# Page registers held longer, index scores packed on the array, and a reordered beginning in a two-layer decoder step

## The chip, the cores and the metric

One NeuronCore of one Trainium2 chip runs the whole program; seven others are idle. The metric is the device time of one execution in microseconds (us). The engines are TensorE (PE in the profile, with PEld for its weight loads), VectorE (DVE), ScalarE (ACT), GpSimd (POOL) and SyncE (SP), which here issues nearly all DMAs.

## The reference, cut to what matters

Two layers work on 544 rows: 512 prompt tokens and 8 samples of 4 new tokens, each sample with 1,024 past tokens in 8 pages of a cache.

```
for l in range(2):
    x += 0.5 * swiglu(rmsnorm(x))              # 1024 -> 2816 -> 1024
    h = rmsnorm(x); z = h @ w_in               # conv, pool, q, k, v, index query qi, index key ki, weights wi
    y_conv = bg * conv3(cg * xin);  y_pool = scale * Wg(windowed means - u)
    score = sum_heads wi * relu(qi . kidx / 8) # 8 index heads of 64, one shared key of 64
    idx = top_k(score, 128 prompt | 256 sample)
    p = softmax(q . k[idx] / 8 + rel_bias[bucket(distance)]);  y_attn = p @ v[idx]
    x += concat(y_conv, y_pool, y_attn) @ w_o
    x += 0.5 * swiglu(rmsnorm(x))
y = rmsnorm(x)   # also returned: the new keys, values, index keys, and conv and pool states
```

All is float32. A large product is three products of rounded parts: `h_hi*w_hi + h_lo*w_hi + h_hi*w_lo`.

## The kernel before

Every engine has its own program in one function; they meet at semaphores, and counters such as `tiles` (steps of PE) order everything. The list `MIX` numbers PE's steps in the mixing part.

**Weights.** SP loads a unit of 512 KB into one of three `raw` slots once the slot's last unit is split; ACT rounds it into `w_hi` (`hi`), POOL subtracts it into `w_lo` (`lo`) and counts `units_split`; six split slots feed PE (`unit_tile`, `product`, L1234). SP's `load` (L358) waits at `units_split`, and POOL gives it the first `RAW_SLOTS` = 3 counts by hand.

**Beginning.** SP loads constants, five row blocks of x, the bias table and one-hot tables. PE transposes x and multiplies the one-hots with the bias table: 12 products on 32 rows (L1338) give the sample bias `bias_s`, two (L1331, L1332) give 639 biases by distance for each of 8 heads. ACT writes those to a DRAM scratch (L656), copied 128 times per head, so that later each of the 128 partitions can read its own shifted row (`strip`, L514). POOL waits for all of PE's beginning (`T_START`) before it hands out the three counts:

```
            pool.wait_ge(tiles, T_START)
            pool.sem_inc(units_split, RAW_SLOTS)
```

Then the norm (statistics on PE, a root on ACT, L966 to L985 on DVE) and the first feed-forward start.

**Mixing part.** After six tiles of z come the index scores. Prompt: 12 tiles `IS` of a query block against the keys, relu on ACT, weighted sums on DVE (L1077, L1080), then top-k of 16 rounds on DVE. Sample: for each of 8 samples PE transposes 8 pages of index keys of 64 columns (`index_keys`, L1402), ACT copies them to `kidxT` (L707), and PE multiplies 3 times (L1416) with 64 contracted rows and 32 output rows. After four samples ACT takes the relu (L711), after eight again (L713), and L1421 sums the heads. PE goes on with 20 tiles of z while DVE runs 32 rounds of top-k for the samples (L1103, L1105), ended by the mask of L1108. PE transposes keys and values to be written out (`NT`, L1471), and then needs that mask in `masks` (L1503).

**Attention** has two halves of four samples each and of eight prompt head pairs. Keys and values arrive in chunks of four pages (1 MB; `chunk`, L438) in a ring of six. Each page number is read from SBUF into a register of SP first (`page_of`, L433); `HELD` = 4 chunks of them are read ahead in the z part and used for keys and values, those of the other chunks are read when needed, twice. `key_tile` (L1491) transposes a key chunk, `logits` (L1512) multiplies, `values` (L1543) takes a value chunk; between them stand the prompt's logits (L1566, L1569), transposes (L1578) and outputs (L1588). In SP's program stand, in this order: key chunks 0 to 4, the outputs of new keys and values (L495 to L502), a wait for all of them to land, since their staging `kn_stage` lies in ring slot 5, key chunks 5 to 7, the 8 `strip` loads, value chunks 0 to 3, a wait for the pool and conv tails and their 7 output DMAs (L526 to L533), value chunks 4 to 7, and the second half. DVE's `p_low` (L1187) writes over the tails' staging, so it waits until these DMAs have landed.

Of the kernel before, what the change touches and what calls it, by code (L numbers as in the profile page):

```python
# [32 lines left out]
P = 128  # L33
# [29 lines left out]
NTD, NTP = LS + DT - 1, SEQ + P - 1  # L63

# [51 lines left out]
MIX = ['STATS', 'ST'] + Z_TILES[:6] + ['WT'] + [f'IS{n}' for n in range(12)]  # L116
MIX += [f'KIT{b}' for b in range(DB)] + ['SC'] + Z_TILES[6:18] + ['TL0', 'PM0'] + Z_TILES[18:]
MIX += ['KIN'] + [f'NT{n}' for n in range(5)]
HALF = NPG
HELD = 4  # L120
for _g in range(2):
    _n0 = HALF * _g
    MIX += [f'KT{_n0}A', f'KT{_n0}B']
    for _i in range(HALF - 1):
        MIX += [f'KT{_n0 + _i + 1}A', f'KT{_n0 + _i + 1}B']
    MIX += [f'NEWL{_g}'] + ['PM1', 'TL1'] * (_g == 0) + [f'PL{_n0}', f'PL{_n0 + 1}', f'PTR{_g}', f'PTN{_g}']
# [19 lines left out]
S_IN = 3 + 5 * DEPTH  # L146


def trunk(nc, a):

    ctx = ExitStack()
    with ctx:
# [50 lines left out]
        kn_stage = at("kn_stage", [P, 4, WA], r_wlo + 8192)  # L203
        oh = at("oh", [32, NTD + NTP], r_whi)
# [4 lines left out]
        kipages = at("kipages", [P, DB, NPG, ID], r_q)  # L209
# [22 lines left out]
        kidxT = at("kidxT", [ID, 2, LS], r_vn)  # L232
# [10 lines left out]
        qis = at("qis", [ID, DB, 32], region(1024))  # L243
# [4 lines left out]
        rel_sb = at("rel_sb", [32, NH], region(32))  # L248
        relx = at("relx", [32, DT, P], r_wlo + 4096)
# [104 lines left out]
        def _(sp):  # L354
# [8 lines left out]
            def index_pages(l, b, pgs):  # L363
                for pg in pgs:
                    page = sp.value_load(pt_sb[0:1, ds(b * NPG + pg, 1)], min_val=0, max_val=last_page)
                    sp.dma_start(kipages[:, ds(b, 1), pg, :].rearrange("p o d -> p (o d)"), a['cache_kidx'][l, page, :, :]).then_inc(kidx_loaded, 16)

            def ffn(l, f):
# [13 lines left out]
                if f == 0:  # L382

                    with sp.Fori(0, DB) as j:
                        gate_up(j + 1, j, 4)
                        hold(sp, "sp", tiles, tile0(l, 0) + 1)
                        index_pages(l, j, range(0, NPG // 2))
                        down_rows(j, j, 8)
                        index_pages(l, j, range(NPG // 2, NPG))
                with sp.Fori(0 if f else DB, FB - 1) as j:  # L390
# [15 lines left out]
            sp.dma_start(rel_sb[:, :], a['rel_bias']).then_inc(s_in, 16)  # L406
# [11 lines left out]
            sp.dma_start(oh[:, :], a['onehots']).then_inc(s_oh, 16)  # L418
# [21 lines left out]
            with sp.Fori(0, DEPTH) as l:  # L440
# [51 lines left out]
                k_chunk(0, 4)  # L492

# [18 lines left out]
                for h in range(NH):  # L512
                    src = bass.AP(a['scratch'].tensor, h * P * NTP + P - 1, [[NTP - 1, P], [1, SEQ]])
                    sp.dma_start(strip[:, h, :], src).then_inc(strip_loaded, 16)  # L514

                for i in range(HALF):
# [7 lines left out]
                    if i == 3:  # L524
                        hold(sp, "sp", tail_done, l * 6 + 6)
                        sp.dma_start(a['pool_prompt'].rearrange("l b t (j c) -> l (b t) j c", c=P)[l, :, :, :], tail_st[0:15, :, :]).then_inc(out_small, 16)  # L526
                        for t in range(DT):
                            sp.dma_start(a['pool_sample'].rearrange("l b t (j c) -> l b t j c", c=P)[l, :, 11 + t, :, :],
                                         tail_st[15 + t:15 + t + 4 * DB - 3:4, :, :]).then_inc(out_small, 16)
                        for t in range(2):  # L530
                            sp.dma_start(a['conv_sample'].rearrange("l b t (j c) -> l b t j c", c=P)[l, :, t, :, :],
# [1140 lines left out]
```

## Time and profile before

| what | value |
|---|---|
| median of 3 runs | 2618.8 us (2618.33 to 2627.82) |
| the profiled execution | 2624.86 us, its span 2623.0 us |
| PE busy | 2421.7 us, 92% of the span, mean granted clock 0.952 |
| VectorE, ScalarE, GpSimd busy | 35%, 28%, 35% |
| DMA | 264.58 MB, mean 101 GB/s |

The profile page cuts the span into 40 slices of 65.6 us. PE's digit is 9 in most, but 4 and 7 in the first two, and 6 to 9 in the mixing parts; there the DMA engines' digit goes up to 7. The page is read with the chain of waits (what ended last, step by step), and stretch by stretch with windows, because an average over the span hides which engine is waited for.

### The profile page before, as it was taken

How to read it: one execution, taken by the hardware profiler on the slowest of the kernel's cores; microseconds unless marked ns; L12 is line 12 of the kernel's file. 1: busy time of each engine (PE TensorE's matmuls, PEld its weight loads, DVE VectorE, ACT ScalarE, POOL GpSimd, SP SyncE). 2: the span in 40 equal slices, each digit the busy share in tenths (PEclk: the TensorE clock that was granted, in tenths of full speed). 3: DMA queues.
4: the chain of work that ended last, by engine and by line, in shares of the span. 5: the costliest groups of instructions: out<-in, count | busy, mean ns of one | idle time of the engine just before them, and what ended most of it. 6: DMA issues, size and time to landing. Idle time of an engine off the chain costs nothing.

```text
span 2623.0 us, 52549 instructions
## 1 busy us (share of the span) xinstructions
PE 2421.7 (92%) x19367; PEld 2264.2 (86%) x19371; DVE 924.5 (35%) x1652; ACT 746.2 (28%) x1072; POOL 929.6 (35%) x483
## 2 busy tenths in 40 slices
PE   4799999899968999999989999989997899999997
PEld 2799999869936889999989999986994578999996
DVE  2122222489534222222242222245973332222223
ACT  1322222342233332222242222234223243222223
POOL 0433344317500343344434443331660033344331
PEclk6899999899988999999989999989998799999998
DMA  4433332213467222223313333221236741232221
GB/s 90 106 89 95 95 102 87 61 33 89 144 222 252 84 78 76 87 86 95 96 52 104 96 94 88 88 62 47 73 120 214 264 125 56 89 96 89 79 88 42
DMA packets 333955, 264.58 MB, mean 101 GB/s; under 512 B 34962, under 2 KB 283280, under 8 KB 333808
## 3 DMA queue, kind: packets, MB, share of 16 engines
q1 hardware_dynamic: 332792, 260.27, 32.6%
q10 hardware_dynamic: 1032, 2.62, 0.9%
q8 instruction: 76, 1.25, 0.2%
q14 instruction: 55, 0.45, 0.1%
HBM read 253.12 MB, written 9.89 MB: 100 GB/s over the span
## 4 chain that ended last, share of the span: by engine, by line
PE 86%; SPq 5%; DMA 3%; DVE 2%; issue 2%; ACT 2%; ACTq 0%; DVEq 0%; POOLq 0%
PE ps L1234 76%; DMA raw<-in_ffn_gate 2%; SPq L438 2%; SPq L433 2%; PE ps L1491 1%; PE ps L1416 1%; PE ps L1588 1%; PE ps L1543 1%; PE ps L1578 1%; DVE work_p L1080 1%; PE ps L1569 1%; PE ps L1512 1%; PE ps L1338 0%; PE ps L1402 0%; DVE sq L961 0%
## 5 line engine op out<-in xcount | busy, mean ns | idle before, releaser
L813 POOL TENSOR_TENSOR w_lo<-raw,w_hi 128x1024 fp32r<-128x1024 f32 (+1 forms) x336 | 796.9, 2385 | 1271.0 <-ACT w_hi L583 1267.3
L1234 PE MATMUL ps<-h_hi,w_hi 128*128 128x272 f32 x3904 | 812.5, 289 | 63.6 <-DVE h_lo L985 58.4
L1234 PE MATMUL ps<-h_hi,w_lo 128*128 128x272 f32 x3904 | 807.2, 289 | 0.0
L1234 PE MATMUL ps<-h_lo,w_hi 128*128 128x272 f32 x3648 | 753.9, 289 | 0.0
L1234 PEld LDWEIGHTS ps<-h_hi,w_hi 128*128 128x128 f32 x3904 | 613.2, 190 | 66.5 <-DVE h_lo L985 59.2
L1234 PEld LDWEIGHTS ps<-h_hi,w_lo 128*128 128x128 f32 x3904 | 612.4, 190 | 0.0
L1234 PEld LDWEIGHTS ps<-h_lo,w_hi 128*128 128x128 f32 x3648 | 575.4, 189 | 0.0
L583 ACT ACTIVATE w_hi<-raw 128x1024 fp32r<-128x1024 f32 (+1 forms) x336 | 343.4, 1044 | 249.4 <-DMA raw<-in_ffn_gate 215.3
L999 DVE TENSOR_TENSOR gated<-ps,silu 128x544 f32<-128x544 f32 x88 | 63.7, 724 | 911.6 <-PE ps L1234 911.6
L1011 DVE SCALAR_TENSOR_TENSOR xT<-ps,xT 128x544 f32<-128x544 f32 x352 | 254.9, 724 | 265.5 <-PE ps L1234 263.0
L1234 PE MATMUL ps<-act_hi,w_hi 128*128 128x272 f32 x1408 | 292.3, 289 | 9.5 <-DVE act_lo L1004 9.5
L1234 PE MATMUL ps<-act_hi,w_lo 128*128 128x272 f32 x1408 | 290.4, 288 | 0.0
L1234 PE MATMUL ps<-act_lo,w_hi 128*128 128x272 f32 x1408 | 290.1, 288 | 0.0
L630 ACT ACTIVATE act_hi<-gated 128x544 fp32r<-128x544 f32 x88 | 53.5, 651 | 625.3 <-PE ps L1234 590.0
L1234 PEld LDWEIGHTS ps<-act_hi,w_hi 128*128 128x128 f32 x1408 | 220.5, 189 | 10.4 <-issue 10.4
L1234 PEld LDWEIGHTS ps<-act_lo,w_hi 128*128 128x128 f32 x1408 | 221.3, 189 | 0.0
L1234 PEld LDWEIGHTS ps<-act_hi,w_lo 128*128 128x128 f32 x1408 | 220.2, 189 | 0.0
L624 ACT ACTIVATE silu<-ps 128x544 f32<-128x544 f32 x88 | 55.1, 626 | 338.8 <-PE ps L1234 338.8
L945 POOL TENSOR_TENSOR cat_lo<-cat,h_hi 128x544 fp32r<-128x544 f32 x8 | 10.7, 1342 | 279.3 <-ACT h_hi L787 279.3
L1103 DVE MAX8 top<-work_s 32x8 f32<-32x1032 f32 x64 | 78.3, 1224 | 10.1 <-DVE work_s L1099 1.1
L1115 DVE COPY keysT<-ps 128x1024 f32<-128x1024 f32 x32 | 39.2, 1224 | 108.1 <-PE ps L1491 108.1
L1105 DVE MATCH_REPLACE8 work_s<-top,work_s 32x1032 f32<-32x1032 f32 x64 | 77.1, 1205 | 0.0
(205 smaller groups left out, 1702.6 us busy)
## 6 DMA issues: line engine op xcount, KB each, us to landing
raw<-in_ffn_gate SPq DMA_DIRECT2D x88, 512.0 KB, 3.8
raw<-in_ffn_up SPq DMA_DIRECT2D x88, 512.0 KB, 4.1
raw<-in_ffn_down SPq DMA_DIRECT2D x88, 512.0 KB, 3.4
ring<-in_cache_k SPq DMA_DIRECT2D x128, 256.0 KB, 4.0
ring<-in_cache_v SPq DMA_DIRECT2D x128, 256.0 KB, 3.7
raw<-in_w_in SPq DMA_DIRECT2D x48, 512.0 KB, 3.8
raw<-in_w_o SPq DMA_DIRECT2D x16, 512.0 KB, 4.2
kipages<-in_cache_kidx SPq DMA_DIRECT2D x128, 32.0 KB, 1.8
```

The source lines that it names most:

```text
L433: return sp.value_load(pt_sb[0:1, at_:at_ + 1], min_val=0, max_val=last_page)
L438: sp.dma_start(ring[c % 6][:, q, :], src[l, four[q], :, :]).then_inc(kv_loaded[c % 6], 16)
L583: act.activation(w_hi[:, c % 6, 0:n], raw[:, c % 3, 0:n], ACT.Copy).then_inc(units_hi, 1)
L624: act.activation(halves(silu[:, m, :]), pair(m), ACT.Silu).then_inc(silu_done, 1)
L630: act.activation(act_hi[:, m, :], gated[:, m, :], ACT.Copy).then_inc(acthi_done, 1)
L813: pool.tensor_tensor(w_lo[:, c % 6, 0:n], raw[:, c % 3, 0:n], w_hi[:, c % 6, 0:n].bitcast(F32), ALU.subtract).then_inc(units_split, 1)
L999: dve.tensor_tensor(halves(gated[:, m, :]), pair(2 + m), halves(silu[:, m, :]), ALU.mult).then_inc(gu_done, 1)
L1011: dve.scalar_tensor_tensor(halves(xT[:, c, :]), pair(c % 4), 0.5, halves(xT[:, c, :]), ALU.mult, ALU.add).then_inc(x_updates, 1)
L1103: dve.max(top8[0:32, 0, :], work_s[:, :]).then_inc(topk, 1)
L1105: dve.match_replace(work_s[:, :], top8[0:32, 0, :], work_s[:, :], TAKEN).then_inc(topk, 1)
L1115: dve.tensor_copy(keysT[k % 2][:, 2:4, :, :].rearrange("p c q n -> p c (q n)"), ps[:, 6:8, :]).then_inc(keys_odd, 1)
L1234: ins = pe.matmul(out[:, hf, :], w, x[:, HT * hf:HT * (hf + 1)], start=first and w is w0 and x is xh, stop=last and w is w1)
```

## The change

It has three parts. **SP's queue:** `HELD` is 7; key chunk 5 no longer waits for the outputs, since `kn_stage` moves to `strip`'s place (in `h_lo`), and `strip` waits for them instead; the tails are taken right after `NT` and written out before key chunk 6; the 8 `strip` loads go by 16 partitions of all heads, not by head. **Index scores:** index keys of two samples lie side by side, so 4 transposing steps of 128 columns instead of 8 of 64, put between the prompt's `IS` tiles; then all 24 products in a row on eight parts of the array (two halves of the rows, four quarters of the columns), one after the other in order. The second half of the query is copied to the other row half by 4 more small products. **Beginning:** POOL hands out the three counts before it waits for `T_START`; the scratch gets 23 copies per head instead of 128; the sample bias is 3 products on 128 rows instead of 12 on 32, for which the table and the one-hots are loaded four times, shifted.

```diff
+ROWS = 7 + 16
...
-MIX += [f'KIT{b}' for b in range(DB)] + ['SC'] + Z_TILES[6:18] + ['TL0', 'PM0'] + Z_TILES[18:]
-MIX += ['KIN'] + [f'NT{n}' for n in range(5)]
+for _n in range(12):
+    MIX += [f'KIT{_n // 3}'] * (_n % 3 == 0) + [f'IS{_n}']
+MIX += ['SC'] + Z_TILES[6:18] + ['TL0', 'PM0'] + Z_TILES[18:]
+MIX += ['KIN'] + [f'NT{n}' for n in range(5)] + ['TL1']
...
-HELD = 4
+HELD = 7
...
-        kn_stage = at("kn_stage", [P, 4, WA], r_wlo + 8192)
+        kn_stage = at("kn_stage", [P, 4, WA], r_hlo)
...
-        kipages = at("kipages", [P, DB, NPG, ID], r_q)
+        kipages = at("kipages", [P, 4, NPG, 2 * ID], r_q)
...
-        kidxT = at("kidxT", [ID, 2, LS], r_vn)
+        kidxT = [at("kidxT0", [P, 2, LS], r_vn), at("kidxT1", [P, 2, LS], r_cat)]
...
-            sp.dma_start(rel_sb[:, :], a['rel_bias']).then_inc(s_in, 16)
+            for t in range(DT):
+                sp.dma_start(rel_sb[32 * t:32 * t + 32, :], a['rel_bias']).then_inc(s_in, 16)
...
-            sp.dma_start(oh[:, :], a['onehots']).then_inc(s_oh, 16)
+            for t in range(DT):
+                sp.dma_start(oh[32 * t:32 * t + 32, 0:LS], a['onehots'][:, DT - 1 - t:DT - 1 - t + LS]).then_inc(s_oh, 16)
+            sp.dma_start(oh[0:32, LS:LS + NTP], a['onehots'][:, NTD:NTD + NTP]).then_inc(s_oh, 16)
...
                 k_chunk(0, 4)
+                k_chunk(0, 5)
...
-                hold(sp, "sp", out_nat[0], (l + 1) * 96)
-                hold(sp, "sp", out_nat[1], (l + 1) * 64)
-                k_chunk(0, 5)
+                hold(sp, "sp", tail_done, l * 6 + 6)
+                sp.dma_start(a['pool_prompt'].rearrange("l b t (j c) -> l (b t) j c", c=P)[l, :, :, :], tail_st[0:15, :, :]).then_inc(out_small, 16)
...
                 hold(sp, "sp", s_scr, 16)
-                for h in range(NH):
-                    src = bass.AP(a['scratch'].tensor, h * P * NTP + P - 1, [[NTP - 1, P], [1, SEQ]])
-                    sp.dma_start(strip[:, h, :], src).then_inc(strip_loaded, 16)
+                hold(sp, "sp", out_nat[0], (l + 1) * 96)
+                hold(sp, "sp", out_nat[1], (l + 1) * 64)
+                for u in range(8):
+                    src = bass.AP(a['scratch'].tensor, u * (NTP - 16) + P - 1, [[NTP - 1, 16], [P * NTP, NH], [1, SEQ]])
+                    sp.dma_start(strip[16 * u:16 * u + 16, :, :], src).then_inc(strip_loaded, 16)
...
-            act.dma_start(a['scratch'], tp_sb[:, :].unsqueeze(1).to_broadcast([NH, P, NTP])).then_inc(s_scr, 16)
+            act.dma_start(a['scratch'][:, 0:ROWS, :], tp_sb[:, :].unsqueeze(1).to_broadcast([NH, ROWS, NTP])).then_inc(s_scr, 16)
...
                 for n in range(12):
                     L = (2 + n // 4) * P
+                    if n % 3 == 0:
+                        act.wait_ge(tiles, T(l, f'KIT{n // 3}'))
+                        act.activation(kidxT[n // 6][:, n // 3 % 2, 0:PAST].rearrange("p (a b) -> p a b", a=2), pair(1, P, 512), ACT.Copy).then_inc(kit_done, 1)
...
+            pool.sem_inc(units_split, RAW_SLOTS)
             pool.wait_ge(tiles, T_START)
-            pool.sem_inc(units_split, RAW_SLOTS)
...
             for b in range(3):
-                for t in range(DT):
-                    ins = pe.matmul(ps[:, b, 0:LT], relx[:, t, :], oh[:, DT - 1 - t + LT * b:DT - 1 - t + LT * (b + 1)], start=t == 0, stop=t == DT - 1)
+                ins = pe.matmul(ps[:, b, 0:LT], relx[:, :], oh[:, LT * b:LT * (b + 1)], start=True, stop=True)
...
+                for t in range(3):
+                    for q in range(4):
+                        for g in range(2):
+                            r = slice(64 * g, 64 * g + 64)
+                            ins = pe.matmul(ps[32 * q:32 * q + 32, 3 * g + t, 0:LT], qis[r, q, :], kidxT[q // 2][r, q % 2, LT * t:LT * (t + 1)], start=True, stop=True)
+                ins.then_inc(score_mm, 1)
+                hold(pe, "pe", relu_done, l * 12 + 12)
                 hold(pe, "pe", srelu_done, l * 2 + 2)
...
+                hold(pe, "pe", nat_done, l * 10 + 4)
+                tail(1)
```

Two places show the new order. The first is PE's program in the index stage, from the end of the prompt's `IS` tiles on. Before:

```order
L1402 MATMUL ps<-cst,kipages 64x128 [waits relu_done]
L1402 MATMUL ps<-cst,kipages 64x128 x7
L313 REGISTER_ALU
L1402 MATMUL ps<-cst,kipages 64x128 [waits relu_done]
L1402 MATMUL ps<-cst,kipages 64x128 x7
L313 ISA
L313 ISA [waits wt_done]
L1416 MATMUL ps<-kidxT,qis 32x344 [waits kit_done]
L1416 MATMUL ps<-kidxT,qis 32x344 x2
```

and now:

```order
L1419 MATMUL ps<-ki,qi 128x512 [waits relu_done]
L1419 MATMUL ps<-ki,qi 128x512
L316 ISA
L316 REGISTER_ALU [waits wt_done]
L316 REGISTER_ALU [waits kit_done]
L1430 MATMUL ps<-kidxT_108,qis 32x344 [waits relu_done]
L1430 MATMUL ps<-kidxT_108,qis 32x344 x3
L1430 MATMUL ps<-kidxT_109,qis 32x344 x4
L1430 MATMUL ps<-kidxT_108,qis 32x344 x4
```

The pages' transposes have gone up between the `IS` tiles, and the scores stand in one row with one wait ahead, where each sample's three had waited for that sample's copy.

The second is SP's program after the outputs of new keys and values. Before:

```order
L502 DMA out_k_sample<-kn_last 32x512 [waits nat_done]
L502 DMA out_v_sample<-vn 32x512
L313 ISA
L313 REGISTER_ALU [waits out_nat0]
L433 TENSOR_LOAD pt_sb [waits out_nat1]
L433 ISA x2
```

and now:

```order
L510 DMA out_k_sample<-kn_last 32x512 [waits nat_done]
L510 DMA out_v_sample<-vn 32x512
L316 ISA
L513 ISA [waits tail_done]
L513 DMA out_pool_prompt<-tail_st 15x256
L515 ISA
L515 DMA out_pool_sample<-tail_st 8x256
```

The wait for the outputs to land and the page reads of key chunk 5 are gone from here; the tails' outputs have come up from behind value chunk 3.

## Rows read from the trace of the kernel before

**Rows 1.** the page's chain that ended last, by engine

```profile
PE 86%; SPq 5%; DMA 3%; DVE 2%; issue 2%; ACT 2%; ACTq 0%; DVEq 0%; POOLq 0%
```

**Rows 2.** windows: stretch, its us, busy us (instructions) of each engine, PEclk, DMA share, GB/s

```profile
38.00:84.00 46.00, 0.23 (x2) 0.20 (x2) 4.03 (x4) 4.03 (x5) 5.51 (x3) 0.50 0.53 81
...
131.00:262.00 131.00, 131.00 (x1055) 131.00 (x1055) 33.70 (x47) 28.89 (x36) 49.08 (x21) 1.00 0.31 93
```

**Rows 3.** the chain of waits, first 130 us: start us, us, what

```profile
17.67 12.79 PE ps L1338 x24
...
31.51 48.05 DMA raw<-in_ffn_gate
...
83.81 46.30 PE ps L1234 x357
```

**Rows 4.** DMA queues from 31 to 74 us, then issues with us to landing

```profile
q10 hardware_dynamic: 843, 2.15, 46.3%
...
raw<-in_ffn_gate SPq DMA_DIRECT2D x2, 512.0 KB, 45.2
```

**Rows 5.** the page's DMA issues: KB each, median us from issue to landing

```profile
raw<-in_ffn_gate SPq DMA_DIRECT2D x88, 512.0 KB, 3.8
```

**Rows 6.** timeline of the beginning: start us, us, engine, line, operation, [idle before <-releaser]

```profile
23.99 1.27 ACTq L656 DMA_DIRECT2D bias_by_distance<-tp_sb  x1
...
30.48 1.23 DVE L1043 TENSOR_SCALAR bias_s<-ps 128x1032 f32<-128x1032 f32 x1 [6.25 <-PE ps L1338]
...
38.08 1.35 DVE L978 TENSOR_TENSOR normed<-xT,ps 128x544 f32<-128x544 f32 x2 [2.43 <-PE ps L1267]
```

**Rows 7.** the chain of waits, the mixing stage's own norm of layer 0

```profile
491.98 0.73 DVE normed L978
...
494.36 38.79 PE ps L1234 x288
```

**Rows 8.** timeline of PE, index stage of layer 0, then its last step in layer 1

```profile
547.90 1.03 PE L1402 MATMUL ps<-cst,kipages 128*64 128x128 f32 x8
...
553.28 1.92 PE L1416 MATMUL ps<-kidxT,qis 64*32 64x344 f32 x6
...
572.63 3.63 PE L1421 MATMUL ps<-srelu,wsel 128*32 128x344 f32 x12 [1.21 <-ACT srelu L713]
...
1835.44 3.63 PE L1421 MATMUL ps<-srelu,wsel 128*32 128x344 f32 x12 [1.21 <-ACT srelu L713]
```

**Rows 9.** timeline of VectorE, end of the sample top-k of layer 0

```profile
690.36 0.88 DVE L1108 TENSOR_SCALAR work_s<-work_s 32x1032 f32<-32x1032 f32 x1
```

**Rows 10.** timeline of PE, first half of the attention of layer 0

```profile
707.00 2.57 PE L1503 MATMUL ps<-work_s,cst 32*128 32x512 f32 x6 [1.83 <-ACT vn L743]
...
718.84 1.08 PE L1512 MATMUL ps<-keysT,qz 128*32 128x128 f32 x32
...
733.92 1.94 PE L1491 MATMUL ps<-cst,ring 128*128 128x128 f32 x16 [2.25 <-DMA ring<-in_cache_k]
...
747.33 1.94 PE L1543 MATMUL ps<-ring,pTs 128*32 128x512 f32 x8 [1.73 <-DVE pTn L1139]
...
796.64 4.00 PE L1503 MATMUL ps<-work_s,cst 32*128 32x512 f32 x6
```

**Rows 11.** waits of the mixing part of layer 0: us in total, times, longest

```profile
PE ps L1543 <- DMA ring<-in_cache_v: 9.5, 4, 4.8
...
PE ps L1588 <- DVE cat_lo L1187: 4.3, 1, 4.3
```

**Rows 12.** the chain of waits, one of the eight small steps of four page reads on SyncE

```profile
715.20 0.27 SPq L433
```

**Rows 13.** timeline of SyncE's queue: tails' outputs, then value chunks 4 to 7

```profile
753.87 3.53 SPq L528 DMA_DIRECT2D out_pool_sample<-tail_st  x4
...
763.54 16.18 SPq L438 DMA_DIRECT2D ring<-in_cache_v  x16
```

**Rows 14.** windows, end of that half (columns as in rows 2)

```profile
784.00:797.00 13.00, 10.91 (x57) 6.00 (x50) 1.76 (x5) 1.81 (x5) 0.00 (x0) 0.50 1.02 367
```

More of the change, by code:

```diff
@@ L145 @@
 OUT_SMALL = 10
-S_IN = 3 + 5 * DEPTH
+S_IN = DT + 2 + 5 * DEPTH
 def trunk(nc, a):
@@ L361, in k_rows, with index_pages @@
                 return raw[:, c % 3, :].rearrange("p (k n) -> p k n", k=KC)
-            def index_pages(l, b, pgs):
-                for pg in pgs:
+            def index_pages(l, pg, batches):
+                for b in batches:
                     page = sp.value_load(pt_sb[0:1, ds(b * NPG + pg, 1)], min_val=0, max_val=last_page)
-                    sp.dma_start(kipages[:, ds(b, 1), pg, :].rearrange("p o d -> p (o d)"), a['cache_kidx'][l, page, :, :]).then_inc(kidx_loaded, 16)
+                    sp.dma_start(kipages[:, b % 4, ds(pg, 1), ID * (b // 4):ID * (b // 4) + ID].rearrange("p o d -> p (o d)"),
+                                 a['cache_kidx'][l, page, :, :]).then_inc(kidx_loaded, 16)
             def ffn(l, f):
@@ L1030, in _ @@
             for t in range(DT):
-                for b in range(4):
-                    dve.tensor_copy(relx[:, t, :].rearrange("p (b h t) -> p b h t", b=4, h=NH)[:, b, :, t], rel_sb[:, :]).then_inc(relx_done, 1)
+                r = slice(32 * t, 32 * t + 32)
+                dve.tensor_copy(relx[r, :].rearrange("p (b h t) -> p b h t", b=4, h=NH)[:, :, :, t],
+                                rel_sb[r, :].unsqueeze(1).to_broadcast([32, 4, NH])).then_inc(relx_done, 1)
             for t in range(5):
@@ L1382, in _, with index_keys @@
                 for c in range(4):
-                    ins = pe.matmul(ps[0:ID, 1, 32 * (c + 1):32 * (c + 2)], ident[64:P, 64:P], qi[64:P, c, SEQ:TOK], start=True, stop=True)
+                    pe.matmul(ps[0:ID, 1, 32 * (c + 1):32 * (c + 2)], ident[64:P, 64:P], qi[64:P, c, SEQ:TOK], start=True, stop=True)
+                    ins = pe.matmul(ps[64:P, 1, 32 * (c + 1):32 * (c + 2)], ident[0:ID, 0:ID], qi[0:ID, c, SEQ:TOK], start=True, stop=True)
                 ins.then_inc(tiles, 1)
+                def index_keys(j):
+                    if j == 0:
+                        hold(pe, "pe", kidx_loaded, (l + 1) * 16 * NPG * DB)
+                    else:
+                        hold(pe, "pe", kit_done, l * 8 + 4 + j)
+                    for pg in range(NPG):
+                        ins = pe.transpose(ps[:, 2 + pg // 4, P * (pg % 4):P * (pg % 4) + P], kipages[:, j, pg, :], ident)
+                    ins.then_inc(tiles, 1)
                 for n in range(12):
                     qb, c, L = 1 + n // 4, n % 4, (2 + n // 4) * P
+                    if n % 3 == 0:
+                        index_keys(n // 3)
                     if n >= 2:
```

125 lines of the change are left out of this document (53 added, 72 removed).

## The prediction

> **What bounds the kernel now.** I read the profile page's chain first: it shows whose work the end waits for. PE has 86% of it, SP's queue 5% and DMA 3% [rows 1]. Windows then tell where PE is full and where not: in the feed-forward it is busy in every microsecond at the full clock, but from 38 to 84 us it works 0.23 us [rows 2]. So only what stands on the path outside the large products can be won. There are three such places: the beginning, the index stage, and the first half of each attention.
>
> **The beginning.** The chain [rows 3] has 12.79 us of sample-bias products, later 48.05 us in which a weight load is waited for, until 79.56, and the first weight product at 83.81. Such a load takes 3.8 us as a rule [rows 5]. It took 45.2 us because it ran beside the scratch write: from 31 to 74 us the write's queue moved 843 of its 8 x 128 = 1,024 rows and took 46.3% of the 16 engines' time [rows 4]. That is 843 / 43 = 19.6 rows a us; the write was issued at 23.99 [rows 6]. The Trainium skill (DMA: Bandwidth & Descriptors, section Bandwidth) says that batches of 1 MiB and more reach 75% of peak; this trace does not agree, since 2.15 MB took these 43 us. If that held, the write would not be the culprit, and the beginning would go as in the fourth rival below.
>
> Now 8 x 23 = 184 rows go out, 9.4 us at 19.6 a us. And the first three weight loads are issued behind the x loads, at some 17 us, while the write starts at some 26; three at 3.8 us each have landed by some 28. What is then late is the norm. The bias products are 3 of the 12: 12.79 x 3/12 = 3.2, 9.6 us less. DVE stood 6.25 us waiting for them at its bias copy [rows 6], so 6.25 is all that comes through, behind it are the squares of the norm. Seven more DMAs ahead of the last x blocks take back some 7 x 0.27 = 1.9 (the price of a small operation of SP, [rows 12]). So the norm comes 4.3 us earlier, its first chunk at 33.8 instead of 38.08 [rows 6]. From that step to the first product the mixing part's own norm takes 494.36 - 491.98 = 2.4 us [rows 7]; the splitting of the first two units runs beside it and ends about then. The first product comes at 36.2 instead of 83.81: **47 us less**. Bounds: 32 (loads that move only once the write ends at 36, three of 3.8, and the 4.2 us from landing to product in rows 3, make 52) and 49 (the six-us wait gone without the DMAs' price). From there on PE's own rate decides [rows 2], so it stays won.
>
> **The index stage.** Before, from 547.90 on, transposes of 1.03 us and scores of 1.92 alternate eight times, with two relus, and the head sum ends at 572.63 + 3.63 = 576.26 [rows 8]. Now the 4 transposing steps go between the prompt's tiles. There DVE's sums set the pace. With 1 us for each transposing step and each copy on ACT, and 8 more small DVE copies, stepping through the twelve tiles gives PE's last one 1.9 us and DVE's last sum 1.5 us later (bounds 0 and 8, nothing or all of it exposed). Behind it: 0.7 for a relu to free the banks, 24 scores on eight parts of the array, so three in a row, 1.92, two relus of 1 us behind each other, the head sum of 3.63, and 0.3 of hand-overs: 8.6 instead of 28.4. z goes on at 558.3, **18 us earlier**. That four column parts overlap is seen: 16 logit products of 128 columns take 1.08 us [rows 10], where by the scores' rate (344 columns in 1.92 / 3) one alone takes 0.24, all 3.8. Eight parts at once no row shows.
>
> But 18 isn't the gain. DVE's top-k for the samples, begun once the prompt's sums are in, ends at 691.24 [rows 9], now at 692.7, and `masks` needs it. Before, `masks` began at 707.00, released by ACT's copy at the end of `NT` [rows 10]; that comes at 689 now. So `masks` begins at 692.9: **14.1 us less** a layer, and in front of it stands a new wait of 4 to 5 us. What is queued behind it on PE is all of the attention. And PE starts slow after waits: at the end of the half the granted clock was 0.50, the 1.2 GHz level, over 13 us [rows 14]. The Trainium skill (TensorE: Matmul & The Clock Gate, Part 1) has an idle PE fall to 1.2 GHz; the trace agrees. I charge 1.3 us, half of `masks`' 2.57 [rows 10] (bounds 0 and 3).
>
> **The first half of attention.** PE waits here for SP: 2.25 for key chunk 7 [rows 10], 9.5 in four waits for value chunks, and 4.3 for DVE's `p_low` behind the tails' outputs [rows 11]; 16.1 in all. On SP four value chunks, 16 loads and three sets of page reads, take 16.18 [rows 13]; a set is eight steps of some 0.27 [rows 12], 2.2, so it is 4.6 a chunk with its set. The tails' seven outputs take some 7, four of them 3.53 [rows 13], and stand between value chunks 3 and 4.
>
> After the change, counted from z's earlier end: key chunks 0 to 5 are issued by 686, the new keys and values by 695, the tails (7 us, moved past) by 702, key chunk 6 by 705, chunk 7 with its reads by 709, `strip` by 714, landed by 719. PE needs chunk 7 at about 718, DVE `strip` at 726. Value chunks follow at 4.3 us, as the addresses are ready: 716 to 738 for 0 to 5, 742 for 6, 748 for 7 (eight page reads ahead of it), landed at 752.5. `values` starts at 747.33 [rows 10] less 14.1, plus 1.3, less 2.25, so at some 732.5, and needs 3 us a step where it doesn't wait: chunk 7 at 753. All waits go, the last one just so; I take off 2 for it: **14.1 us**. With them goes the slow clock: 10.91 us of PE work stood at 0.50 [rows 14], half of it is won, some 1.6 more in front of it: **7 us**, bounds 2 and 9. In the second half no wait for a chunk shows; page reads saved there are covered by PE and win nothing.
>
> **The sum.** A layer: 14.1 - 1.3 + 14.1 + 7 = 33.9; layer 1 repeats it, its head sum the same 3.63 [rows 8]: 68. With 47: 115 us. The profiled execution, 2624.86, gives 2509.9; it stands 6.1 over the median of the runs, 2618.8, and inside their spread. For a median I give **2504 us**.
>
> **The rivals.**
> - SP or the DMA engines still set the pace of the values: `strip` and 19 outputs are now all ahead of value chunk 0. For it: chunk 7 has no margin, and from 784 to 797 the engines were full at 367 GB/s [rows 14]. Against: the tails are gone from the middle. If half of the waits for chunks and of the clock's 7 stay, 10 a layer are lost: 2524.
> - The early loads still meet the write: 32 instead of 47, 2519.
> - The eight parts don't overlap, so the change doesn't do what it says: the scores take 8 x 1.92 = 15.4, z is 5 us earlier only, `masks` at 702, 9 a layer are lost: 2522. Against it stand the logits. At a fourfold overlap, 3.8, nothing changes: top-k covers it.
> - The first loads are slow by themselves, with or without the write beside them. Then only their earlier issue counts, 31.5 to 17: 14 instead of 47, 2537. That is what the bandwidth rule of the Trainium skill cited above would make of it. Rows 4 and 5 speak against.
> - Slower than before: with fewer pauses PE isn't granted its full clock in the feed-forward. Work at 1.2 GHz takes twice as long, so each us of full-speed work caught costs 1 us. To end over 0.5% slower it must catch 115 + 13 = 128 us, a mean clock near 0.90 where it was 0.952: 2632 or more. Against: 131 us without a pause at 1.00 [rows 2].
>
> **How the numbers follow.** My own case, 2490 to 2514: 0.62. Pace of the values 0.22, early loads 0.06, scores 0.05, slow loads 0.02, slower 0.01, two of them together 0.02, of which I let half end within 0.5%. The range goes from 2488, all at the good bounds, to 2534, the values' rival with most of the early loads' loss. 0.5%, 13 us, is about what a measurement of this kernel can tell from no change. Faster 0.98, within 0.01, slower 0.01.
>
> **What would show it.** Right: the first weight product near 36 us; `masks` released by DVE's mask after 4 to 5 us of wait; no wait over 2 us for a chunk; from `masks` to `masks` some 70 us instead of 796.64 - 707.00 = 89.6 [rows 10]. Wrong: a first product after 45, over 5 us of waits for values, or scores of much over 4 us.

## The result and the profile after

The changed kernel takes 2531.21 us (median of 4 runs, 2528.0 to 2537.04), the kernel before in the same comparison 2622.53 (4 runs, 2618.33 to 2627.82). The ratio is 0.9653, 95% interval 0.9629 to 0.9677: 3.5% faster. The forecast was 2504 in a range of 2488 to 2534. The sign was right, the time lies 27 us over the forecast and 3 us inside the upper end.

The profiled execution took 2537.04 us, its span 2535.2, 87.8 less than before. First the page: the chain by engine, which answers to [rows 1].

```profile
PE 82%; DVE 10%; issue 5%; ACT 2%; DVEq 1%; DMA 0%; SPq 0%; ACTq 0%
```

SP's queue and the DMAs, 8% before, are gone from the chain. DVE has come in with 10% (the top-k), and "issue", in which an engine waits for nothing that the profile names, has gone from 2% to 5%. Little of that is the stops shown further down, which are 8.2 and 8.4 us of the 2535.2 us span: e1_spread, whose stops are 2.3 and 1.6 us, has 5% as well.

The timeline of the beginning answers to [rows 3] and [rows 6].

```profile
26.71 0.55 ACTq L663 DMA_DIRECT2D bias_by_distance<-tp_sb  x1
26.87 1.23 DVE L1054 TENSOR_SCALAR bias_s<-ps 128x1032 f32<-128x1032 f32 x1
...
34.46 1.35 DVE L988 TENSOR_TENSOR normed<-xT,ps 128x544 f32<-128x544 f32 x2 [2.43 <-PE ps L1281]
...
37.45 0.82 PE L1248 MATMUL ps<-h_hi,w_hi 128*128 128x272 f32 x2 [3.02 <-DVE h_lo L995]
```

The first weight product starts at 37.45 instead of 83.81. What it waits for is DVE's split of the activations, no longer a load.

The timeline of PE in the index stage of layer 0 answers to [rows 8] and the first of [rows 10]: the stage's first product (the weights `wi`), the first step that transposes index keys, the scores, the head sum, and `masks`.

```profile
490.39 0.63 PE L1393 MATMUL ps<-cst,wi 128*128 128x128 f32 x4 [0.81 <-ACT qi L683]
...
491.68 1.09 PE L1407 MATMUL ps<-cst,kipages 128*128 128x128 f32 x8
...
507.31 1.97 PE L1430 MATMUL ps<-kidxT,qis 64*32 64x344 f32 x48
...
511.48 3.63 PE L1436 MATMUL ps<-srelu,wsel 128*32 128x344 f32 x12 [2.20 <-ACT srelu L719]
...
652.76 3.98 PE L1521 MATMUL ps<-work_s,cst 32*128 32x512 f32 x6 [8.43 <-DVE work_s L1122]
```

All 24 score products of 344 columns take 1.97 us, where before three took 1.92: eight ran at a time. The stage's first product stood here before:

```profile
533.94 0.63 PE L1380 MATMUL ps<-cst,wi 128*128 128x128 f32 x4 [0.81 <-ACT qi L676]
```

The head sum ends 24.7 us after the stage's first product (515.11 - 490.39) instead of 42.3 (576.26 - 533.94). But `masks`, now released by DVE, starts 162.4 us after it instead of 173.1, and PE has stood 8.43 us.

The chain of waits in the first attention half of layer 0, where [rows 10] and [rows 11] had SP and its loads:

```profile
677.35 0.77 PE ps L1530 x19
678.12 5.77 issue
683.89 1.07 PE ps L1530 x13
...
691.39 2.47 issue
```

No wait for a value chunk is left. Instead PE stops twice in the middle of a row of products, for 5.77 and 2.47 us, and the profile names nothing that it waits for. Layer 1 has two such stops of 2.75 and 5.63 us. Windows show what else is going on at 676 to 684 us (columns as in [rows 2]).

```profile
676.00:684.00 8.00, 2.23 (x36) 1.80 (x38) 1.23 (x1) 1.02 (x1) 0.00 (x0) 0.87 1.08 130
```

The DMA engines are busy all the time and move 130 GB/s. At the end of the half [rows 14] they were as busy at 367 GB/s. Under way are the eight loads of `strip`, issued from 668.6 to 672.7 us, each now 16 neighbouring partitions with all heads, and the first value loads, queued behind them. From issue to landing the `strip` loads of both layers took (minimum, median, maximum), in the trace before and then in the one after:

```profile
DMA to landing us min/median/max: 3.5/4.5/5.5
```

```profile
DMA to landing us min/median/max: 6.9/12.9/18.9
```

Laid out along the execution, the gain of the two profiled executions reads so (PE's first row of each place):

| stretch | before, us | after, us | gain | forecast |
|---|---|---|---|---|
| start to first weight product | 83.81 | 37.45 | 46.4 | 47 |
| to the index stage of layer 0 | 450.1 | 452.9 | -2.8 | 0 |
| index stage to `masks`, layer 0 / 1 | 173.1 / 173.1 | 162.4 / 162.3 | 10.7 / 10.8 | 14.1 each |
| `masks` to `masks`, layer 0 / 1 | 89.6 / 89.4 | 77.7 / 77.8 | 11.9 / 11.6 | 19.8 each |
| all the rest | 1563.9 | 1564.7 | -0.8 | 0 |
| span | 2623.0 | 2535.2 | 87.8 | 115 |

### The profile page after: what moved, and what is told of

Its sections match the earlier page's. It is cut to its first block, busy times and chain, and to the rows that moved or that the text cites. A ratio compares the mean times of both kernels' runs of the same rounds, so it can differ in the third digit from the quotient of the medians.

```text
span 2535.2 us, 52176 instructions
## 1 busy us (share of the span) xinstructions
PE 2380.4 (94%) x19301; PEld 2252.6 (89%) x19305; DVE 921.2 (36%) x1658; ACT 736.5 (29%) x1056; POOL 929.2 (37%) x483
## 4 chain that ended last, share of the span: by engine, by line
PE 82%; DVE 10%; issue 5%; ACT 2%; DVEq 1%; DMA 0%; SPq 0%; ACTq 0%
PE ps L1248 69%; DVE work_s L1119 3%; DVE top L1117 3%; PE ps L1509 3%; PE ps L1561 1%; PE ps L1530 1%; PE ps L1606 1%; PE ps L1587 1%; PE ps L1596 1%; DVE work_p L1110 1%; DVE sq L971 1%; DVE top L1108 1%; PE ps L1521 1%; PE ps L1419 0%; PE ps L1584 0%
## 5 line engine op out<-in xcount | busy, mean ns | idle before, releaser
L955 POOL TENSOR_TENSOR cat_lo<-cat,h_hi 128x544 fp32r<-128x544 f32 x8 | 10.7, 1344 | 270.2 <-ACT h_hi L797 270.2
L1509 PE MATMUL ps<-cst,ring 128*128 128x128 f32 x512 | 72.8, 303 | 1.1 <-DVE keysT L1129 1.0
```

What stands on the lines that cost most here:

```text
L1509: ins = pe.transpose(ps[:, 4 + c4, P * q:P * (q + 1)], ring[c % 6][:, q, P * c4:P * (c4 + 1)], ident)
```

## The experiments

Theory A was: 16 neighbouring partitions are a slow place to load to, and while those loads fill the DMA engines PE runs out of instructions. Its rivals: the small scratch tensor is read over and over, or the change only shifted waits. All experiments start from the changed kernel or from e1_spread. e2, e3, e9 and e10 were run once each, the others four times.

### Spread partitions: e1_spread

```
-    src = bass.AP(scratch, u * (NTP - 16) + P - 1, [[NTP - 1, 16], [P * NTP, NH], [1, SEQ]])
-    sp.dma_start(strip[16 * u:16 * u + 16, :, :], src)
+    src = bass.AP(scratch, P - 1 - u, [[NTP - 8, 16], [P * NTP, NH], [1, SEQ]])
+    sp.dma_start(strip[u:P:8, :, :], src)
```

> The changed kernel with one edit: each of the 8 strip loads writes partitions u, u+8, ..., u+120 instead of 16 neighbours (from 16 rows of the scratch, since every row is the same). Theory A, neighbours: 16 neighbouring partitions take data slowly, that is why the strip loads took 6.9 to 18.9 us to land (4.5 before the change) with all DMA engines at 100% and only 130 GB/s, and that starved PE of its instructions (waits of 5.8 and 2.5 us named issue). Then landing falls to 4 to 6 us, both issue waits fall under 1 us, the first half of the attention goes from 77.8 to about 69, and the kernel to about 2531 - 17 = 2514. Theory B, the small scratch: reading 1,024 rows out of a few hundred KB is slow; with 16 rows it is at least as slow, landing stays over 12 us and the time at 2531.

2520.62 us (2516.71 to 2524.97, 4 runs), ratio to the kernel before 0.9613, 0.9594 to 0.9633. Every run is faster than every run of the changed kernel. The bytes, the loads and their number are the same; only the partitions of one load differ. The strip lands after 6.9 us in the median, and the waits of PE in this half of layer 0 are:

```profile
PE ps L1521 <- DVE work_s L1122: 6.7, 1, 6.7
PE ps L1539 <- issue: 2.3, 1, 2.3
PE ps L1561 <- DMA ring<-in_cache_v: 1.9, 1, 1.9
```

So theory A holds in its first half. It falls short of what was expected, 10.6 us instead of 17: an issue wait and a wait for a chunk are left, and so is a slow clock, below. It has the lowest time of this study and beats both kernels; only the median of e6, below, lies within its spread.

### How many rows, which partitions: e2, e9, e10, e5

Four more kernels fill the table of layouts. The edits are `ROWS = P` (e2, e9, e10) with each partition reading its own row, and the form of the loads:

```
e2:   strip[16 * u:16 * u + 16, :, :]   16 neighbours, 8 heads
e10:  strip[u:P:8, :, :]                16 spread, 8 heads
e9:   strip[:, h, :]                    128 partitions, one head, as before
e5:   strip[:, h, :]                    the same with 23 rows: [[NTP - 16, 8], [NTP - 1, 16], [1, SEQ]]
```

> The changed kernel with the scratch back at 128 rows a head; the strip loads still go by 16 neighbouring partitions, each from its own row. Theory A (neighbouring partitions are slow): strip landing stays at 7 to 19 us and the issue waits stay. Theory B (the small scratch is slow to read): landing 4 to 6 us, issue waits gone. At the beginning: the first three weight loads are still issued at 18 us, before the write, so the first product should stay near 37.5, but the fourth load and those behind it meet the write, which now runs to some 80 us; I expect PE to stop for some 30 us in the first feed-forward (first stage over 20 us longer).

> The strip exactly as in the kernel before (head by head, 128 partitions, each partition from its own row of the scratch tensor, so 128 rows are written again), everything else as in the changed kernel. It costs the first FFN some 22 us, as e2_rows128 showed, so only the attention is to be read. While the strips land, the kernel before moved about 320 GB/s, the changed kernel 125, e2 (16 neighbouring partitions, 128 rows) 135, e1 (16 spread partitions, 23 rows) 205, e5 (128 partitions, 23 rows) 200. Theory A1 (the partitions alone decide): as e5, about 200 GB/s and DVE waiting over 4 us for the strip. Theory B1 (two effects: neighbouring partitions, and reading few rows over and over): about 300 GB/s, no wait of DVE for the strip over 1 us, no wait of PE for instructions, and a first attention half of 71 us or less in layer 0 (e1 74.4, e5 76.5).

> As e1_spread (16 spread partitions, eight heads a load), but each partition from its own row, 128 rows written; the first FFN loses some 22 us again. It is the fourth cell beside e1 (205 GB/s), e2 (135) and e9. If few rows are what held e1 at 205 GB/s, it is near 300 GB/s here and the strips land after about 4.5 us (7.2 in e1). If the shape of the load (16 partitions with eight runs of 2 KB each) is what costs, it stays at 200 GB/s and 7 us.

> This is e1_spread with the strip again loaded head by head: eight loads of 128 partitions and one head each, as in the kernel before, but out of the 23 rows. Theory A (what matters is how many different partitions one load writes, so 128 is better than 16 spread ones, and those better than 16 neighbouring ones): a strip load lands after a median of about 4.5 us as in the kernel before (6.9 in e1_spread, 12.5 in the changed kernel), PE's wait for instructions before the new logits (2.33 us in e1_spread) shrinks under 1 us, and the time is 1 to 4 us under e1_spread's 2520.6, so 2517 to 2520. Theory B (the loads are slow because all eight read the same 23 rows of the scratch tensor): landing stays near 7 us or above, and the time stays within 1 us of e1_spread's. Theory C (the saturation comes from strip and 32 chunks together, 2 MB beside the values, whichever partitions are written): landing falls but the issue wait stays at 2 us.

Windows of 8 us, each from 5 us after the first strip load of layer 0, in this order: before, changed kernel, e2, e1, e10, e9, e5.

```profile
736.10:744.10 8.00, 4.93 (x113) 3.62 (x103) 3.41 (x12) 3.85 (x9) 0.00 (x0) 1.00 1.02 377
```

```profile
673.60:681.60 8.00, 4.52 (x75) 3.73 (x74) 2.45 (x2) 2.05 (x2) 0.00 (x0) 1.00 1.08 129
```

```profile
697.50:705.50 8.00, 6.81 (x104) 5.82 (x103) 2.45 (x2) 2.51 (x3) 0.00 (x0) 1.00 1.08 138
```

```profile
669.20:677.20 8.00, 7.73 (x137) 6.56 (x135) 3.61 (x3) 3.08 (x3) 0.00 (x0) 1.00 1.07 211
```

```profile
697.00:705.00 8.00, 7.68 (x136) 6.51 (x134) 3.65 (x3) 3.08 (x3) 0.00 (x0) 1.00 1.07 206
```

```profile
696.50:704.50 8.00, 7.78 (x137) 6.62 (x135) 3.56 (x3) 3.07 (x3) 0.00 (x0) 1.00 0.99 349
```

```profile
669.70:677.70 8.00, 7.71 (x137) 6.54 (x134) 3.62 (x3) 3.08 (x3) 0.00 (x0) 1.00 0.87 185
```

| partitions of one load | 128 rows | 23 rows |
|---|---|---|
| 16 neighbours | 138 GB/s | 129 |
| 16 spread | 206 | 211 |
| 128, one head | 349 (before: 377) | 185, engines at 0.87 |

With 16 partitions the number of rows makes no difference, so rereading a small scratch isn't the cause there. Which partitions a load writes does make one: with full engines 130, 210 and 350 GB/s. The Trainium skill (SBUF — State Buffer, Door 1: The DMA port swizzle) says that DMA bandwidth depends on how many of SBUF's 16 DMA ports the partitions reach, and gives the bits of the partition number that choose the port. By that, 16 neighbours reach 4 ports, every eighth partition 8, and 128 all 16; by its 435 GB/s over 16 ports that would be some 109 and 218 GB/s, an estimate. The measured 206 to 211 agree; the 129 to 138 lie higher, with key and value loads to all partitions beside them. I didn't weigh that page in the prediction.

e5, expected to be the best, is a miss: 2529.19 us (2523.6 to 2531.87, 4 runs), 8.6 over e1. Here the engines weren't full. From 667 to 671 us, with nearly only strip loads under way, their share was 0.57:

```profile
667.00:671.00 4.00, 4.00 (x74) 3.46 (x76) 1.51 (x2) 1.97 (x2) 0.00 (x0) 1.00 0.57 171
```

Its source pattern begins with a dimension of 8, where e9's begins with 128. The Trainium skill (DMA: Bandwidth & Descriptors, Why a DMA increments its semaphore by 16 and not by 1) has a queue use the largest number of engines up to 16 that divides the outermost dimension of both sides, which gives 8 of 16; the share of 0.57 agrees. The scratch write of the kernel before, whose pattern begins with its 8 heads, had 46.3% of the engines' time [rows 4]. But e5 differs from e9 in two things, the pattern and the 23 rows, and no run parts them. DVE waited 5.7 us for the strip in e5, while PE had no issue wait: these slow loads, on engines that weren't full, came with none. In e9, with 16 engines and 128 partitions, the loads landed after 4.1, 4.7 and 6.9 us, DVE didn't wait, and PE's one issue wait was 0.9 us. So layout and issue waits go together in layer 0: 8.2 us at 129 GB/s and 7.1 at 138 (e2), 2.3 at 211 and at 206 (e10), 0.9 at 349.

The attention half doesn't follow them all the way. The three kernels with 128 rows differ in the layout alone, and the shortest halves are e10's:

| kernel | GB/s | first half, layer 0 / 1 | PE's issue waits | PE's waits for value chunks | clock in the last 14 us |
|---|---|---|---|---|---|
| e2 | 138 | 76.1 / 76.4 | 7.1 / 7.2 | 0 / 0 | 0.90 / 1.00 |
| e10 | 206 | 70.1 / 69.5 | 2.3 / 2.0 | 0 / 0.8 | 1.00 / 1.00 |
| e9 | 349 | 73.7 / 75.4 | 0.9 / 0 | 2.7 / 4.3 | 0.58 / 0.50 |

e9 was expected at 71 us or less and missed. Its faster loads took away the stops, but value chunks came late instead, and the clock fell.

The totals of e2, e9 and e10 (2554.33, 2552.07 and 2542.53 us, one run each) are spoilt by the 128 rows at the beginning. In e2 the first product comes at 37.31, as in the changed kernel, but the index stage starts at 514.43. The waits of PE in the first feed-forward say why:

```profile
PE ps L1248 <- POOL w_lo L823: 22.1, 1, 22.1
```

The weight loads issued from 30 to 70 us took 40.6 and 42.3 us (medians of the two kinds). The stop of 22.1 us was expected at some 30. The early issue saved the first product, and a later unit paid: the price of the write moves, it does not go, until the write is small.

### Loads held back again: e3_held

```
-            pool.sem_inc(units_split, RAW_SLOTS)
             pool.wait_ge(tiles, T_START)
+            pool.sem_inc(units_split, RAW_SLOTS)
```

> The changed kernel with POOL's three counts handed out only after T_START again, the scratch at 23 rows. Loads are issued at about 27 us, together with a write that takes some 9 us. Theory write (the load waits for the write, whatever its size): first units land at 36 to 42, first product at 42 to 46, 5 to 8 us later than 37.45. Rival, first loads slow by themselves: first product beyond 60.

One run, 2535.67 us, inside the spread of the changed kernel. The first product starts at 37.39, against 37.45: a miss. The loads go out at 23.99 instead of 17.89, beside a write of 192 packets, and are there in time anyway. So of the beginning's 46.4 us nothing needs the early loads. What counts is that the write has shrunk to 23 rows.

### What is left of the waits: e4, e6, e8, e11

e4_keys_last puts the four transposing steps of the index keys behind the twelve prompt tiles, so that DVE's sums, and with them the top-k, end earlier. e6_strip_later issues the strip behind the second value chunk. e8_both has both. e11_strip_halves loads the 256 columns that the first half needs first, the others in the second half.

```
e4:   MIX += [f'IS{n}' for n in range(12)] + [f'KIT{n}' for n in range(4)]
e6:   v_pages(0, i)
      if i == 1: the 8 strip loads
e11:  strip_part(256) in their old place, strip_part(0) behind k_chunk(1, 3)
```

> e1_spread with the four steps that transpose index keys moved behind the twelve prompt tiles (two PSUM pairs in turn). Top-k bounds the start of masks, so what delays DVE's sums counts and what delays PE does not, as long as PE still waits. DVE's last sum comes 3.1 us earlier in the stage, the head sum some 2.3 us later, the wait for DVE's mask falls from 8.4 to about 3 us, masks start 3 us earlier a layer: 6 us less than e1_spread, about 2508. Rival, PE's own work bounds: no gain or a loss against e1_spread.

> This is e1_spread with the eight strip loads behind the second value chunk in SP's queue instead of ahead of the first. Their first user is a DVE operation at 684.5 us in e1_spread, against an issue at 664 to 669, so they have some 10 us to spare. Expected if SP's queue order is what sets the value chunks: the wait of 1.9 us for a value chunk in layer 0 (0.9 in layer 1) goes, and the time falls 1 to 3 us under e1_spread's 2520.6. If the bytes are what sets them (the DMA engines were busy all the time from 665 to 685 us), nothing is gained: within 1 us of 2520.6. If the strip comes too late, DVE waits for it at about 684 us and PE's prompt logits with it: 2 to 5 us slower a layer.

> This is e4_keys_last (index keys transposed after the twelve score tiles) with the strip loads behind the second value chunk as in e6_strip_later. e4_keys_last had its masks 2.1 us earlier a layer and lost 4 to 6 us behind them; its PE waited 5.8 us in three pieces for value chunks there. If those chunks were late because they stand behind the strip in SP's queue, this kernel keeps the earlier masks: the waits for value chunks fall under 2 us a half, and the time is at or under e1_spread's, 2514 to 2520. If the bytes set the pace, the waits stay near 5.8 us and the time near 2531.

> e1_spread with the strip in two parts: its last 256 columns, which are all that the eight query tiles of the first attention half use, where the strip was loaded before; its first 256 columns behind the fourth key chunk of the second half, where DVE waits for them at its ninth tile. So 1 MB instead of 2 MB stands ahead of the value chunks at 664 us. If the time a strip takes goes by bytes, the DMA engines get free some 4 us earlier, PE's wait for instructions (2.3 and 1.6 us) and for a value chunk (1.9 and 0.9) go, and the time is 3 to 7 us under e1_spread's 2520.6. If it goes by the number of pieces (1024 in either part), nothing is gained at 664 us and the second part is 1024 pieces more: 0 to 4 us slower. A wait of DVE for the second part at about 730 us would show as well.

| kernel | median (runs), us | masks after index start | first half, layer 0 / 1 | PE's wait for chunks, layer 0 |
|---|---|---|---|---|
| e1 | 2520.62 (4) | 162.3 | 74.4 / 69.1 | 1.9 |
| e4 | 2531.41 (4) | 160.2 | 78.5 / 74.8 | 5.8 |
| e6 | 2523.40 (4) | 162.3 | 74.3 / 69.3 | 2.3 |
| e8 | 2531.93 (4) | 160.2 / 161.8 | 79.3 / 78.3 | 3.7 |
| e11 | 2527.17 (4) | 162.3 | 74.0 / 75.5 | 3.9 |

None beats e1; e6 can't be told from it. e6 has no issue wait any more, but DVE waits 5.8 us for the later strip and PE 2.4 for DVE: the wait changes its name. In e8 DVE waits 9.5 and 10.9 us for the strip, and the chunk waits, expected under 2, are 3.7 and 1.9. e11 cuts the bytes in half, not the pieces; its strip lands after 4.9 us and PE has no issue wait over 0.2, yet PE waits 3.9 and 4.0 us for value chunks, the last 14 us of both halves stand at 0.50 and 0.51, and it is 6.6 us slower than e1. e4 does bring `masks` 2.1 us forward and pays 4 to 6 us a half for it. Its PE had 2.3 us of wait for the top-k instead of 6.7, and this is what it lost. In SP's queue the outputs of the new keys and values stand ahead of key chunk 6, and they can't go before PE has transposed them. In e1 they begin 7.9 us ahead of `masks` (640.66 against 648.53), in e4 only 3.4 (646.12 against 649.52), and key chunk 6 goes out 12.2 us behind `masks` instead of 7.8. So PE's wait for the top-k is time in which SP gets ahead.

### The parts undone: e7 and e13

e7_queue_undone is e1 with the rest of the SP part taken back: tails behind value chunk 3, key chunk 5 behind the outputs, `HELD = 4`. e13_scores_undone is e1 with the index stage of the kernel before.

```
e7:   -HELD = 7                              +HELD = 4
e13:  -    MIX += [f'KIT{_n // 3}'] * (_n % 3 == 0) + [f'IS{_n}']
      +MIX += [f'KIT{b}' for b in range(DB)] + ['SC']
      +ins = pe.matmul(ps[r:r + 32, t, 0:LT], qis[:, b, :], kidxT[:, b % 2, LT * t:LT * (t + 1)])
```

> This is e1_spread with the rest of the SP part undone: the eight small outputs behind the fourth value chunk again, key chunk 5 behind the outputs of keys and values, and four page numbers handed out ahead instead of seven. The strip stays in eight spread loads out of 23 rows. It prices the SP part of the change with the beginning and the scores left in. My prediction gave 14.1 us a layer to all waits of the first attention half, of which a wait for value chunks of 4 to 9.5 us each (27 us in two halves of the kernel before). Expected: the waits for value chunks come back with 5 to 12 us a layer, the masks stay where they are in e1_spread (648.5 us), and the time is 2530 to 2545, that is 10 to 24 us over e1_spread. Rival: the eight strip loads and the earlier masks already removed those waits, and the order of outputs was worth under 2 us a layer: within 4 us of 2520.6.

> e1_spread with the index stage of the kernel before: keys of one batch at a time on 64 partitions, scores four at a time, key transposes behind the twelve score tiles. Beginning, SP queue and the spread strip stay as in e1_spread, so it prices the index part alone. From the traces: the head sum ended 17.3 us after the later head-weight product more than in the changed kernel (576.26 - 533.94 against 515.11 - 490.39), but DVE's sums over the prompt tiles ended 3.1 us earlier there, and the top-k chain sets the masks. My prediction took 14.1 us a layer; the changed kernel's masks came 10.6 us (layer 0) and 12.6 us (layer 1) earlier beyond the beginning's gain. Expected by the trace: the masks 10 to 14 us later a layer than in e1_spread (162.3 us after the index weights' first row there, so 173 to 176 us), a first attention half 0 to 5 us shorter a layer because the value chunks are then always there, and 2533 to 2546 in all, 12 to 25 us over e1_spread's 2520.6. Rival: the masks move, but SP's queue and the DMA engines set the pace behind them, and the attention half gives nearly all of it back: under 6 us in all.

e7: 2547.52 us (2538.84 to 2553.01, 4 runs), ratio 0.972, 0.9698 to 0.9743; 26.9 over e1, a little more than expected. `masks` comes at 650.67 (162.3 after the index start, as in e1), the halves are 79.2 and 82.1 us, and the wait for value chunks is back with 9.0 and 6.5 us.

e13: 2561.36 us (2558.43 to 2562.61, 4 runs), ratio 0.9765, 0.9749 to 0.9781; 40.7 over e1, where I expected 12 to 25. `masks` is 10.8 us later a layer (173.1), as the traces had said. But the halves, expected 0 to 5 us shorter, grew to 79.2 and 79.0 us, with the beginning and the whole new queue in place. The waits of PE in this half of layer 0:

```profile
PE ps L1554 <- DMA ring<-in_cache_v: 9.1, 5, 3.6
...
PE ps L1514 <- ACT vn L750: 1.5, 1, 1.5
```

PE doesn't wait for the top-k here. It runs straight into `masks`, at 662.93, and the outputs begin at 660.22, 2.7 us ahead of it. The rows of SP's timeline, e1 and then e13: key chunks 6 and 7.

```profile
656.34 7.44 SPq L445 DMA_DIRECT2D ring<-in_cache_k  x8
```

```profile
675.65 7.44 SPq L442 DMA_DIRECT2D ring<-in_cache_k  x8
```

That is 7.8 us after `masks` in e1 and 12.7 in e13, and every value chunk behind them is that much later. So the packed scores do two things: 10.8 us a layer by themselves, and a first half shorter by 4.8 us in layer 0 and by 10 in layer 1. That the second comes of PE finishing its outputs while DVE still sorts is read from the order of SP's queue in e4 and e13; no run moved the outputs alone. The two parts are not additive: 26.9 for the queue, 40.7 for the scores and 46.4 for the beginning make 114, the whole of e1 is 102 us under the kernel before.

## Why the prediction was right and where not

- **The beginning**, 47: right, 46.4, and by the mechanism (the 184 rows). The norm's first chunk came at 34.46 where I had 33.8. The part "loads at some 17 us" gave nothing (e3). Of the gain 2.8 us were gone by the index stage of layer 0. From 37.5 to 50 us the changed kernel had a granted clock of 0.76, where the kernel before had 0.87 in its first 12.5 us (84.0 to 96.5). Some of it differs from execution to execution: from 450 to 490 us the changed kernel had 0.92 and e1, whose program is the same up to there, 0.99, and e1 reached the index stage at 486.27 instead of 490.39.
- **The head sum 18 us earlier**: right, 17.6; the eightfold overlap, which no row of before showed, is there with 1.97 us for 24 products.
- **"`masks` begins at 692.9: 14.1 us less a layer"**: 10.7. The term that was mis-sized is DVE's. Its last prompt sum comes 3.1 us later in the stage, not 1.5 (20.5 after the stage's first product, 17.5 before). 1.5 more come from a single small operation in the chain, in both layers. It takes 0.15 us in the trace of before, and in the trace of after it ends when GpSimd's does (both timelines):

```profile
600.08 0.15 DVE L1099 TENSOR_TENSOR work_s<-work_s,cst 32x8 f32<-32x8 f32 x1
```

```profile
559.60 1.61 DVE L1113 TENSOR_TENSOR work_s<-work_s,cst 32x8 f32<-32x8 f32 x1
```

```profile
558.79 2.40 POOL L823 TENSOR_TENSOR w_lo<-raw,w_hi 128x1024 fp32r<-128x1024 f32 x1 [0.34 <-ACT w_hi L590]
```

  It ends at 561.21, GpSimd's split at 561.19. The Trainium skill (SBUF — State Buffer, Who interferes with whom) says that a DVE instruction with two inputs from SBUF contends with a GpSimd instruction that reads SBUF; these rows agree. In the twelve kernels with the new index stage this operation takes 1.5 to 1.6 us in 21 of 24 layers, each time to the end of a split by GpSimd. In layer 1 of e7, e8 and e9 it falls outside a split and takes 0.14 to 0.15, and in e7 and e9 `masks` then comes 160.8 us after the stage's first product instead of 162.3. One row doesn't fit: in e8 it lies inside another GpSimd operation that reads SBUF and still takes 0.15. So the 1.5 us hang on GpSimd's split; by which mechanism isn't shown.
- **A wait of "4 to 5 us" ahead of `masks`**: 8.4 and 6.8. PE was ready a little earlier than I had it, and DVE 3.4 later. **`masks` at the slow clock**, 1.3: it took 3.98 instead of 2.57, 1.4.
- **"All waits go", 14.1, and the clock, 7**: the step that failed. All waits for SP and for chunks did go, and `p_low`'s. "`strip` by 714, landed by 719" was wrong: I took the five us of the old loads for new ones of the same size. They took up to 18.9 us, the DMA engines gave 130 GB/s, and PE stood 8.2 us (layer 1: 8.4) in issue waits. 19.8 a layer less 8.2 is 11.6; measured 11.9 and 11.6. In layer 0 two smaller errors cancel in that: 16.1 us of waits went, not 14.1, and what is left for the clock is some 5.4, not 7 (11.9 + 8.2 + 1.4 - 16.1). The rival on the pace of the values had the size nearly right, 10 a layer, but another mechanism: no value chunk was late.
- **The clock.** Its 7 us can be read across all runs. In most halves the last 14 us stood at 0.50 to 0.60 or at 0.9 to 1.0. In e1, layer 0 and layer 1, the latter of 69.1 us, which is what I had forecast:

```profile
709.00:723.00 14.00, 10.78 (x57) 5.84 (x57) 2.62 (x8) 2.92 (x10) 0.00 (x0) 0.55 1.02 372
...
1941.70:1955.70 14.00, 10.99 (x99) 5.50 (x91) 6.26 (x26) 6.55 (x21) 0.00 (x0) 1.00 0.92 325
```

  Nearly the same busy time holds 57 matmul records in the one stretch and 99 in the other. In the changed kernel these stretches had 1.00 and 0.91: there the clock's gain had come, and the issue waits took it. Over the 28 halves of all 14 kernels one thing goes with the level: the ten in which PE waited under 1 us in all for value chunks had a granted clock of 0.90 or more in their last 14 us, and of the 18 with 1.9 us or more of such waits 15 had 0.68 or less (not layer 1 of e4, and not e7). That is seen in the rows, not a cause shown. It goes some way to say why e9 and e11, whose strip loads landed sooner than e1's, have no shorter halves.
- The terms against the sum: index -6.7, halves -16.1, feed-forward and rest -3.5, beginning -0.6 make the 27 us that separate 115 from 87.8.
- That 2531 lies inside the range is luck. The upper end, 2534, was set by two rivals together, neither of which held, and PE's stops stood in none of them.
- Of the other rivals none held: the early loads didn't meet the write, the eight parts overlap, and the feed-forward had the clock it had before.

Open: that PE "runs out of instructions" is a reading; the profile names no releaser. Shown is that these waits shrink with the layout of the loads alone, from 8.2 to 2.3 us at 23 rows and from 7.1 to 2.3 to 0.9 at 128. The traces hold more for it. They have a DMA queue of the kind "instruction". In the changed kernel it moves one packet in 680 to 681 us and one in 691 to 692:

```profile
q8 instruction: 1, 0.02, 10.3%
```

```profile
q8 instruction: 1, 0.02, 6.9%
```

Each execution has 76 such packets of 16 KB, and all 19 issue waits of PE over half a us behind the beginning, in eight kernels, end 1.3 to 1.9 us after one of them has ended (here 682.40 and 692.51, against 683.89 and 693.86). The stops also come at the same places of the program: those of L1530 leave 13 records of its row, those of L1539 one. Whose instructions the packets hold the profile doesn't say. Not tried: ordering the spread loads so that two neighbours in the queue fall on different ports, and e5's layout with an outermost dimension of 16.

## What to carry to other kernels

A load of few partitions isn't priced by its bytes: look at which partitions it writes and at the outermost dimension of its patterns, in the window's GB/s beside its DMA share. Here a full DMA share at a third of the rate was the layout, not the traffic. The fastest layout still didn't give the shortest attention: e10, at 206 GB/s, had shorter halves than e9 at 349. And before a wait is counted as loss, look at who uses it: here PE's pause for the top-k let the output queue get ahead, and shortening the pause lengthened the attention.

## What was not expected of the hardware

- Loads to 16 neighbouring partitions ran at 129 to 138 GB/s with all DMA engines busy, to every eighth partition at 206 to 211, to 128 partitions at 349 to 377.
- 128 partitions through a source pattern with an outermost dimension of 8 (and 23 rows): a DMA share of 0.57.
- PE stopped up to 5.8 us (7.2 in e3) in the middle of a row of products while the DMA engines were full at a low rate, and went on 1.3 to 1.9 us after a 16 KB packet of the instruction queue.
- A 32 x 8 VectorE operation took 1.61 us instead of 0.15, ending with GpSimd's own operation, and 0.14 to 0.15 where it fell outside GpSimd's split.
- Twenty-four products of 64 rows by 32 columns and 344 wide took 1.97 us on eight parts of the array.
